# Low parts of the early tiles on GpSimd: four operations of 512 elements a tile in place of two of 1024

## The reference

```python
q = (xt @ w_query).reshape(T, 8, 2, 128)             # 8 heads, two halves each
scores = einsum('thpc,hpnc->thpn', q, sub_keys)      # 128 keys per half
top_s, top_i = lax.top_k(scores, 16)                 # 16 best of 128, per half
cand_s = top_s[:, :, 0, :, None] + top_s[:, :, 1, None, :]   # sums of pairs
best_s, best_pos = lax.top_k(cand_s, 16)             # 16 best pairs
idx = take_along_axis(cand_i, best_pos, axis=-1)     # the chosen experts
gate = softmax(best_s)
act = gelu(einsum('cd,ced->ce', xc, u)); y = einsum('ce,ced->cd', gate * act, v)
```

## Time and profile before

| | |
|---|---|
| median of three runs | 3100.95 us |
| span of the profiled execution | 3093.4 us, 53809 instructions |
| what lies around the span, by the median | 7.55 us |
| TensorE (PE) busy | 2988.8 us, 97% |
| VectorE (DVE) busy | 1920.4 us, 62% |
| ScalarE (ACT) busy | 1347.9 us, 44% |
| GpSimd (POOL) busy | 132.4 us, 4%, of which 124.0 us in the 52 low-part operations |
| mean granted TensorE clock | 0.989 |

### The profile page before, as it was taken

The page is one execution under the profiler, slowest core; times in us unless marked ns, Lnnn a source line. Parts: engine busy times, 40 slices in busy tenths (PEclk is TensorE's granted clock), DMA queues, the critical chain, the costliest instruction groups (busy, mean ns, idle before and its releaser), DMA issues. The chain is left out here.

```text
span 3093.4 us, 53809 instructions
## 1 busy us (share of the span) xinstructions
PE 2988.8 (97%) x20906; PEld 2608.6 (84%) x20906; DVE 1920.4 (62%) x3659; ACT 1347.9 (44%) x2053; POOL 132.4 (4%) x62
## 2 busy tenths in 40 slices
PE   8998999999999999999999999999998999999898
PEld 7697889899898869888989989887777979777797
DVE  4489864787647648986478764755534564543546
ACT  4442444444444544244444444445424444442444
POOL 0061000000000006100000000000000000000000
PEclk9999999999999999999999999999999999999999
DMA  5243354544555424335454455553234545223444
GB/s 214 93 180 123 123 191 177 193 154 155 190 183 197 164 97 171 128 135 191 178 192 147 163 190 194 186 191 123 96 136 150 189 178 214 73 96 136 156 185 150
DMA packets 68022, 493.59 MB, mean 160 GB/s; under 512 B 7576, under 2 KB 7584, under 8 KB 8352
## 3 DMA queue, kind: packets, MB, share of 16 engines
q1 hardware_dynamic: 67568, 490.42, 43.6%
q0 software_dynamic: 304, 1.06, 0.1%
HBM read 490.39 MB, written 1.06 MB: 159 GB/s over the span
## 5 line engine op out<-in xcount | busy, mean ns | idle before, releaser
L780 DVE TENSOR_TENSOR ring_l<-ring,tile_h 128x1024 fp32r<-128x1024 f32 x648 | 765.0, 1222 | 667.9 <-ACT tile_h L735 663.8
L735 ACT ACTIVATE tile_h<-ring 128x1024 fp32r<-128x1024 f32 x644 | 645.7, 1051 | 533.2 <-PE ps L666 445.3
L634 PE MATMUL ps<-x_h,tile_h 128*128 128x256 f32 x2016 | 575.5, 285 | 2.1 <-issue 2.1
L635 PE MATMUL ps<-x_l,tile_h 128*128 128x256 f32 x2016 | 570.0, 283 | 0.0
L636 PE MATMUL ps<-x_h,ring_l 128*128 128x256 f32 x2016 | 569.9, 283 | 0.0
L634 PEld LDWEIGHTS ps<-x_h,tile_h 128*128 128x128 f32 x2016 | 386.4, 192 | 3.1 <-issue 2.8
L635 PEld LDWEIGHTS ps<-x_l,tile_h 128*128 128x128 f32 x2016 | 386.5, 192 | 0.2
L636 PEld LDWEIGHTS ps<-x_h,ring_l 128*128 128x128 f32 x2016 | 386.3, 192 | 0.0
L739 ACT ACTIVATE arena<-ps 128x512 f32 (+1 forms) x160 | 95.6, 597 | 432.2 <-PE ps L636 346.5
L664 PE MATMUL ps<-tile_h,w_even 128*128 128x512 f32 x640 | 249.5, 390 | 3.6 <-DVE w_even L805 3.6
L664 PE MATMUL ps<-tile_h,w_odd 128*128 128x512 f32 x640 | 249.3, 390 | 0.6 <-DVE w_odd L805 0.6
(11 more groups left out here) (322 smaller groups left out, 5598.8 us busy)
## 6 DMA issues: line engine op xcount, KB each, us to landing
ring<-stream SPq DMA_DIRECT2D x464, 1024.0 KB, 4.8
cs<-consts SPq DMA_DIRECT2D x1, 1712.5 KB, 8.6
x<-x_in SPq DMA_DIRECT2D x1, 1024.0 KB, 5.1
arena<-scratch POOLq DMA_DIRECT2D x1, 1024.0 KB, 7.8
out<-x SPq DMA_DIRECT2D x2, 512.0 KB, 2.7
tab<-table SPq DMA_DIRECT2D x1, 1.0 KB, 8.4
scratch<-arena POOLq DMA_DIRECT2D x1, 12.0 KB, 5.0
```

What stands on the lines that cost most here:

```text
L634: nc.tensor.matmul(out, uh[:, c, f], x_h[:, c, :], start=(c == 0), stop=False)
L635: nc.tensor.matmul(out, uh[:, c, f], x_l[:, c, :], start=False, stop=False)
L735: nc.scalar.activation(tile_h[:, j % 2, n], slot(k + j)[:, n], ACT.Copy).then_inc(hi_ready, 1)
L780: nc.vector.tensor_tensor(low_of(k + j)[:, n], slot(k + j)[:, n], tile_h[:, j % 2, n].bitcast(F32), ALU.subtract).then_inc(lo_ready, 1)
```

## The change

Each low part of an early tile is written in four operations of 512 elements, each counted in `el_ready`; the first two still wait for the first half of the high part, the last two for the second. TensorE waits for `el_ready` ahead of chunks 0, 2, 4 and 6.

```diff
@@ pe_early
-                    if c % 4 == 0 and fb == 0:
-                        pe.wait_ge(el_ready, l * (2 * AHEAD) + (2 * n + c // 4 + 1))
+                    if c % 2 == 0 and fb == 0:
+                        pe.wait_ge(el_ready, l * (4 * AHEAD) + (4 * n + c // 2 + 1))
@@ pool_early_lows
-                for hf in range(2):
-                    part = slice(1024 * hf, 1024 * hf + 1024)
-                    pool.wait_ge(eh_ready, l * (2 * AHEAD) + (2 * n + hf + 1))
+                for q in range(4):
+                    part = slice(512 * q, 512 * q + 512)
+                    pool.wait_ge(eh_ready, l * (2 * AHEAD) + (2 * n + q // 2 + 1))
                     nc.gpsimd.tensor_tensor(low_of(k)[:, part], slot(k)[:, part], early_h[n % 3][:, part].bitcast(F32),
                                             ALU.subtract).then_inc(el_ready, 1)
```

## The result

The changed kernel takes **3104.16 us** (median of 17 runs, 3098.2 to 3112.72); the kernel before, run beside it, 3100.19 us (17 runs, 3092.39 to 3103.14). The ratio is 1.0018, with a 95% interval of 1.001 to 1.0026: 3 to 8 us more. The forecast was 3102.8 us and "no change", with a range to 3106.5. So the time lies in the range and within what was called no change. The rest of this text shows that the sum of +1.8 us had the right mechanism and came out near 0, and that the 4 us measured go with something it did not hold, the clock that TensorE was granted.

The account below looks back on a forecast made before the run. TensorE, busy 97% of the span, was held to wait for VectorE's chain, stalled by GpSimd. Terms 0 and +1.8 us made the span 3095.2; with 7.55 around it, 3102.8 us, range 3094 to 3106.5.

Parts of the forecast that it names:

- the sum of +1.8 us: Whole kernel: 0 for TensorE's added waits plus +1.34 us in layer 0 and +0.47 in layer 1 for VectorE's chain.
- 52 more waits on TensorE: Ahead of early tiles' products: no price, since GpSimd stays ahead of TensorE; 1.7 us to spare at tile 3.
- d = 1.30 us: Length of one 512-element low part on GpSimd, taken midway between 1.23 and 1.385 us.
- The walk: VectorE's pair additions, head by head, against GpSimd's low parts: one passes at each end; +1.34 and +0.47 us by layer.
- Rival A: Layer 0: head 6 of VectorE's chain begins before GpSimd's tile 12; 6.4 to 9.0 us shorter in all; 14%.
- B: VectorE's stalls behind GpSimd halve, from 32.05 to 16 us, giving 3085 us; 5%.
- C: GpSimd's low parts have 0.5 us fixed and last 1.43 us; 6.6 us later, 3107.5 us and more; 5%.
- 7.55 us around the span: Time outside the profiled span, added to the forecast span of 3095.2 us to reach 3102.8 us.

Follow-up runs that it names:

- e2: Kernel before with only TensorE's four waits per tile; GpSimd's low parts stay in two operations that count double: 3101.12 us, 0.9988 to 1.0015 against before.
- the eighths: Changed kernel with eight low parts of 256 elements a tile, products waiting for each: 3121.5 us, 1.0052 to 1.0086 against before.
- c_before: The kernel before, unchanged, run and profiled once more: 3102.13 us median of 12 runs.
- e1: Kernel before with only GpSimd's low parts cut into four operations, TensorE waiting as before: 3102.66 us, 1.0000 to 1.0023 against before.
- e4: Changed kernel with the second block left out: 2026.89 us, against 2024.07 us for the kernel before cut the same way.
- e7: Changed kernel plus eight unused 128x512 products on TensorE, which ran three times: 3105.48 us, 1.0004 to 1.0029 against before.
- e11: Changed kernel with GpSimd's four operations cut to 16 elements each, high part used in place of the low part: 3083.5 us, 0.9928 to 0.9964 against before.
- e8: Kernel before plus eight unused 128x512 products on TensorE: 3103.94 us, 0.9987 to 1.0021 against before.
- e5: Changed kernel with four and five expert tiles split early in layers 0 and 1 in place of seven: 3085.44 us, 0.9935 to 0.9967 against before.
- e6: Kernel before, low parts in halves, with four and five expert tiles split early in place of seven: 3100.54 us, 0.9984 to 1.0014 against before.

## Why the prediction was right, step by step

- **52 more waits on TensorE, 0 us.** Right, as far as this can be measured: the list of TensorE's waits has no row with POOL after either, and e2, which has them alone, shows before's waits and a ratio of 0.9988 to 1.0015.
- **d = 1.30 us.** Measured 1.255, between the 1.23 that I held for the least and what I took. The fixed part of an operation is 2 x 1.255 - 2.37 = 0.14 us, not the 0.23 that 1.30 implies; the eighths confirm it (33.5 us for 48 gives 0.70 each). The 4497 ns for 2048 elements in the Trainium skill ("GPSIMD Engine Reference", Performance versus the Vector engine) had led to an estimate of 0.33 fixed and d near 1.36: too much here. The walk at 1.26 gave +0.1 us, at 1.30 +1.8; so +1.8 is the term that was mis-sized.
- **The walk.** Right in kind. Its rule, with d = 1.255 and tile times of the executions with the low clock near 158 us, puts head 7's first addition at 250.64 (seen: 250.63), and with halves within 0.2 us of the 251.37 seen in c_before. Like against like TensorE's waits differ by +0.20 and -0.40 us, so what the shorter waits give is returned at the end of the run, as forecast (one pair of executions; e1's and e4's traces lie higher in layer 1). Wrong in detail: head 0 meets no tile in these executions, and in layer 0 heads 2, 3, 5 and 6 stall in place of 0, 2, 4, 5 and 6. Incomplete too: it has neither the four that pass at one end (e7, some 2.3 us gained) nor the one that is held (5 us and more lost). The walk rested on one execution, and the meeting of heads and tiles differs from one to the next.
- **Rival A** needed d of 1.22 or less; it was missed by 0.035 us, and would have been a gain. **B** needed several additions at one end as the usual case: with quarters and GpSimd at work throughout, that was seen at one head, in e7. **C** needed 1.43.
- **The sum against the median.** The text set 7.55 us around the span; the lists show some 1.8. The profiled execution plus the +1.8 us of the sum would have been 3097.0; that the sum was hung on the median was sound, but the reason given was wrong. That the forecast of 3102.8 us lies within 1.4 us of the 3104.16 measured is in part luck: the walk's +1.8 came out near 0, and the clock, which is in no term, filled its place.
- **Where the 4 us are.** Not in a term of the sum. The means are 3100.6 (106 runs of halves) and 3104.2 us (37 of quarters). The 31 runs of halves at a clock of 0.988 or more average 3094.0, the other 75 3103.3; the 36 others of quarters 3104.4. So 2.5 of the 3.7 us are the missing runs at the higher clock, (31/106 - 1/37) x 9.3, and 1.1 are in the rest. A line through all 143 runs gives -2.4 us per 0.001 of clock and, at equal clock, 0.0 us (standard error 0.4) for the quarters. The line says what goes with the clock and not what causes it: the clock is the mean of the whole execution, and the waits that the change touches move it too. In the 16 us behind layer 0's wait it is 0.86 in before (284 to 300 us), 0.91 in the changed kernel (281 to 297), and 1.00 in e11, which has no wait (270 to 286).
- **What stays open.** Why the kernel with quarters gets the higher clock so seldom: e1 against e2 (0 of 11, 4 of 12) suggests, with few runs, that it goes with GpSimd's pieces and not with TensorE's waits, and e7 and e8 that a later second block does not undo it; beyond that nothing is shown. And how often an addition is held in the changed kernel: 2 of 6 profiled executions with quarters (e4, e7), in none of six with halves. Since one costs 5 to 7 us, it is a candidate for the 1.1 us, no more.

## What to carry to other kernels

Before cutting one engine's operations to let another through, ask what happens to the total: here GpSimd's work got longer (124.0 to 131.2 us), each wait shorter, and the number of waits rose by as much. What helped was to make the run that is met shorter and its pieces too (e5, five runs, in part by the clock); shorter pieces alone did not, nor, in the median, a shorter run alone (e6). And compare like with like before a gain or a loss is read from two traces: a low clock near 158 us made 4 us of "gain", and the stretch from 2087 to 2117 us with its low clock 10 us of "loss", with no instruction changed at either place. And count in the trace how often an edit runs: the eight products of e7 and e8 ran three times.

## What the runs showed that was not expected

- **An addition can be held over many ends.** 9.86 and 11.11 us with quarters, 26.41 and 18.05 us with eighths, each until GpSimd's uninterrupted run was over; none in the six profiled executions with halves, whose longest addition is 2.47 us. Which of three things happens to a head (one per end, all four at one end, none until the run is over) decides over -2 to +6 us. The Trainium skill says that the ports shared by the two engines are locked for a whole instruction ("SBUF — State Buffer", SBUF: two separate sides); the 1.31 us additions agree. It does not say which engine is next when both wait, and these four waited for many instructions. Where in GpSimd's operation the addition arrives does not tell them apart: 0.32 us into one it was held in e4 (1237.83) and passed in the changed kernel (1237.12).
- **The clock of a few narrow products is worth more than the change.** At L1614 it makes 5.75 us (13.08 less 7.33) in one execution against another, and 4.26 us (11.59 less 7.33) between two executions of one unchanged kernel, whose runs spread from 3090 to 3113 us.
